# Last expert quad brought back to features as well as rows, its overflow branch moved ahead of it, and two weight splits moved ahead of the convolution's taps

## The reference

```python
def hierarchical_moe(h, ...):              # end of the first layer
    a = jnp.einsum('sd,edf->sef', hr, w_gate)
    u = jnp.einsum('sd,edf->sef', hr, w_up)
    act = jax.nn.silu(a) * u * gate[:, :, None]
    return jnp.einsum('sef,efd->sd', act, w_down)

def hybrid_layer(x, ...):                  # the second layer
    h = rmsnorm(x, g_mix)
    z = h @ w_in
    rnn_x, rnn_y, conv_b, conv_c, conv_x, gate_rnn, gate_conv = jnp.split(z, IN_OFFSETS, axis=-1)
    rnn_x = causal_depthwise_conv(rnn_x, conv4_w) + conv4_b
    y_rnn = jax.nn.gelu(rnn_y) * rg_lru(rnn_x, w_rg_r, b_rg_r, w_rg_i, b_rg_i, lru_lambda)
    y_conv = conv_b * causal_depthwise_conv(conv_c * conv_x, conv3_w)
    merged = jax.nn.sigmoid(gate_rnn) * y_rnn + jax.nn.sigmoid(gate_conv) * y_conv
    x = x + merged @ w_out
```

## Time and profile before

| | us |
|---|---|
| median of 3 runs | 854.52 |
| lowest, highest | 853.46, 856.09 |
| the profiled execution | 852.39 |
| its span, first to last instruction | 850.6 |

### The profile page before, as it was taken

How to read it: one execution, slowest core, us unless ns; L and a number is a source line. 1 busy time by engine, 2 the same in 40 slices (tenths; PEclk the granted TensorE clock), 3 DMA queues, 4 the chain that set the end, 5 groups by cost and what they waited for, 6 DMA issues and landing times.

```text
span 850.6 us, 13779 instructions
## 1 busy us (share of the span) xinstructions
PE 802.4 (94%) x5546; PEld 656.0 (77%) x5546; DVE 493.6 (58%) x832; ACT 416.1 (49%) x708; POOL 20.1 (2%) x41
## 2 busy tenths in 40 slices
PE   9999999999999976788879999999999999999996
PEld 7888888888965543444349899999988888888886
DVE  6667777865542110110047899898976555555486
ACT  5777488666411100100246757575746344444466
POOL 1700000000000000000000000000000000000000
PEclk9999999999999988989999999999999999999999
DMA  9855533977899999999984847465574665655521
GB/s 323 270 192 186 174 112 99 342 300 297 302 384 424 423 425 422 425 423 424 417 284 154 268 127 245 149 221 168 203 253 155 221 188 196 197 170 185 188 99 50
DMA packets 95184, 214.47 MB, mean 252 GB/s; under 512 B 4728, under 2 KB 59552, under 8 KB 81824
## 3 DMA queue, kind: packets, MB, share of 16 engines
q1 hardware_dynamic: 93456, 211.70, 68.3%
q0 software_dynamic: 1376, 1.89, 0.8%
q10 hardware_dynamic: 304, 0.20, 0.1%
HBM read 212.72 MB, written 1.05 MB: 251 GB/s over the span
## 4 chain that ended last, share of the span: by engine, by line
PE 62%; DVE 12%; SPq 11%; DMA 7%; issue 4%; ACT 3%; DVEq 1%; ACTq 0%
PE bank L2212 13%; PE bank L2214 13%; PE bank L2213 13%; SPq L829 11%; DMA embed<-in_expert_w_down_dram 4%; PE bank L2229 4%; PE bank L2225 3%; PE bank L2722 3%; DVE w_lo L455 2%; DVE w_lo L453 2%; PE bank L2219 2%; PE bank L2220 2%; DMA stage<-in_w_in_dram 2%; PE bank L2759 2%; DMA whole<-in_expert_w_down_dram 1%
## 5 line engine op out<-in xcount | busy, mean ns | idle before, releaser
L2212 PE MATMUL bank<-w_hi,xT_hi 128*128 128x512 f32 (+2 forms) x390 | 150.9, 387 | 0.0
L2214 PE MATMUL bank<-w_hi,xT_lo 128*128 128x512 f32 (+2 forms) x390 | 148.5, 381 | 0.0
L2213 PE MATMUL bank<-w_lo,xT_hi 128*128 128x512 f32 (+2 forms) x390 | 148.2, 380 | 0.0
L2954 PE MATMUL bank<-hT_hi,w_hi 128*128 128x256 f32 x440 | 122.2, 278 | 1.7 <-DVE w_lo L455 1.0
L2955 PE MATMUL bank<-hT_lo,w_hi 128*128 128x256 f32 x440 | 121.5, 276 | 0.0
L2956 PE MATMUL bank<-hT_hi,w_lo 128*128 128x256 f32 x440 | 121.5, 276 | 0.0
L453 DVE TENSOR_TENSOR w_lo<-stage,w_hi 128x1024 fp32r<-128x1024 f32 (+3 forms) x78 | 87.8, 1126 | 29.5 <-ACT w_hi L439 28.5
L439 ACT ACTIVATE w_hi<-stage 128x1024 fp32r<-128x1024 f32 (+3 forms) x80 | 78.6, 983 | 26.9 <-PE bank L2214 13.3
L455 DVE TENSOR_TENSOR w_lo<-stage,w_hi 128x1024 fp32r<-128x1024 f32 (+3 forms) x78 | 87.6, 1123 | 0.0
L2954 PEld LDWEIGHTS bank<-hT_hi,w_hi 128*128 128x128 f32 x440 | 82.6, 188 | 2.9 <-DVE w_lo L455 2.1
L2214 PEld LDWEIGHTS bank<-w_hi,xT_lo 128*128 128x128 f32 x390 | 73.3, 188 | 14.2
(11 more groups left out here) (485 smaller groups left out, 1603.2 us busy)
## 6 DMA issues: line engine op xcount, KB each, us to landing
stage<-in_w_in_dram SPq DMA_DIRECT2D x36, 1024.0 KB, 5.4
stage<-in_w_gate_up_dram SPq DMA_DIRECT2D x44, 512.0 KB, 4.7
whole<-in_expert_w_up_dram SPq DMA_DIRECT2D x11, 1024.0 KB, 26.0
stage<-in_w_down_dram SPq DMA_DIRECT2D x11, 1024.0 KB, 4.8
whole<-in_expert_w_gate_dram SPq DMA_DIRECT2D x9, 1024.0 KB, 24.9
stage<-in_w_out_dram SPq DMA_DIRECT2D x8, 1024.0 KB, 5.3
stage<-in_cross_w_kv_dram SPq DMA_DIRECT2D x7, 1024.0 KB, 8.7
whole<-in_expert_w_down_dram SPq DMA_DIRECT2D x6, 1024.0 KB, 23.4
```

The lines of the kernel that those rows point to most:

```text
L2212: mm(o, k_hi, v_hi, start=start, stop=False)
L2213: mm(o, k_hi, v_lo, start=False, stop=False)
L2214: return mm(o, k_lo, v_hi, start=False, stop=stop)
L2954: mm(o, w_hi[:, s, at:at + P], hT_hi[:, k, :], start=k == 0, stop=False)
```

## The change

- The rows' sums of quads 0 to 6 are copied to `x` right after quad 6, turned by `turn_sums` between gates and ups of quad 7, and stay in banks 0 to 3. Quad 7's output is multiplied into those turned banks (`add_turned`: `y` as weights, `token_now` moving, 256 columns) and, apart, into rows in banks 6 and 7 (`rows_back`), which DVE adds to `x` (`add_rows`).
- Banks 0 to 3 then hold the features, so `turn("mix", ...)` goes, and `hT_hi`, `hT_lo` come from them (`mix_high`, `mix_low`). The order of ACT, DVE and PE in the join is written anew. `last_rows` puts the second half of the rows inside `highs_first`.
- The overflow branch and its flag's load go in front of quad 7 on every engine; on SP the head's first three loads come behind it. The four products by `zeros` in it go.
- `x` and `raw_turned` change places in the ring, and units 13 and 20 change order in SP's program.
- In the heads' loop on DVE, `unit(RG_I)` and `unit(G_R)` are put ahead of the `conv3` work and of its second and third taps.

```diff
@@ SP
-        load_expert(sp, 20)
+        load_expert(sp, 13)
         sp.wait_ge(sem("norm_sums"), nth(NORMS, "moe"))
         sp.wait_ge(sem("x_kept"), 4)
-        load_expert(sp, 13)
+        load_expert(sp, 20)
...
-        sp.wait_ge(sem("gates_done"), QUAD * QUADS)
-        for j in range(RING):
-            load_head(0, j)
         with sp.If(over_flag > 0):
...
+        sp.wait_ge(sem("gates_done"), QUAD * QUADS)
+        for j in range(RING):
+            load_head(0, j)
@@ ACT
+        def mix_high(n):
+            act.wait_ge(sem("mix_turned"), n + 1)
+            for j in range(2):
+                k = 2 * n + j
+                ins = nc.scalar.activation(hT_hi[:, k], bank[n][:, 256 * j:256 * j + 256], ACT.Copy, scale=gain_of(MIX_G, k))
+            ins.then_inc(sem("xT_hi"), 1)
...
-        high_parts("mix", MIX_G)
+        down_high(QUADS - 1, 0)
+        mix_high(0)
+        mix_high(1)
+        for t in range(T):
+            mix_squares(0, t)
+        down_high(QUADS - 1, 1)
+        first_columns_hi(0)
+        mix_high(2)
+        mix_high(3)
         first_columns_hi(1)
         split_hi(act, SLOT, U_HEADS + 1)
-        mix_squares(0, 0)
-        mix_squares(0, 1)
         mix_squares(1, 0)
         mix_squares(1, 1).then_inc(sem("norm_sums"), 1)
@@ DVE
+        down_low(QUADS - 1, 0)
+        mix_low(0)
+        mix_low(1)
+        add_rows(0)
+        down_low(QUADS - 1, 1)
+        first_columns_lo(0)
+        mix_low(2)
+        mix_low(3)
         first_columns_lo(1)
+        add_rows(1)
         split_lo(dve, SLOT, U_HEADS + 1)
...
             link(stt(y_in[:], y_tanh[:], 1.0, y_in[:], ALU.add, ALU.mult))
+            unit(RG_I)
...
             for f in range(2):
                 ins = ts(conv3[:, f], cpad[:, f, 0:256], col(conv3_w, 0, f), None, ALU.mult)
+            unit(G_R)
             for tap in range(1, 3):
...
             link(ins)
-            unit(RG_I)
-            unit(G_R)
             unit(G_C)
@@ PE
+        def turn_sums():
+            pe.wait_ge(sem("sums_copied"), 4)
+            view = x[:].rearrange("p t (k q) -> p t k q", k=KD)
+            for n in range(4):
+                for j in range(2):
+                    for t in range(T):
+                        mm(bank[n][:, 256 * j + P * t:256 * j + P * t + P], view[:, t, 2 * n + j], ident, start=j == 0 and t == 0, stop=False, is_transpose=True)
+
+        def add_turned(c, y, low):
+            for n in (2 * c, 2 * c + 1):
+                for j in range(2):
+                    at = 256 * n + P * j - 512 * c
+                    ins = mm(bank[n][:, 256 * j:256 * j + 256], y[:, c, at:at + P], token_now[:].rearrange("p t s -> p (t s)"), start=False, stop=low and j == 1)
+                if low:
+                    ins.then_inc(sem("mix_turned"), 1)
...
+        last = QUADS - 1
+        quad(last)
+        pe.wait_ge(sem("embed_copied"), 4)
+        down(last, 0)
+        pe.wait_ge(sem("token_now"), QUADS)
+        pe.wait_ge(sem("expert_y_hi"), 2 * last + 1)
+        add_turned(0, y_hi, False)
+        rows_back(0, y_hi, False)
+        pe.wait_ge(sem("expert_y_lo"), 2 * last + 1)
+        add_turned(0, y_lo, True)
+        rows_back(0, y_lo, True)
+        down(last, 1)
+        pe.wait_ge(sem("expert_y_hi"), 2 * last + 2)
+        add_turned(1, y_hi, False)
+        pe.wait_ge(sem("expert_y_lo"), 2 * last + 2)
+        add_turned(1, y_lo, True)
...
-        turn("mix", x, [("x_moe0", 1), ("x_moe1", 1)], (0, 1))
-        turn("mix", x, [("x_moe0", 2), ("x_moe1", 2)], (2, 3))
```

More of the change, by code:

```diff
@@ L1355, in expert_quad, with down_high @@
             nc.scalar.activation(hiddenT[:].rearrange("p k s -> p (k s)"), bank[7][:, 0:2 * P], ACT.Copy).then_inc(sem("hidden_copied"), 1)
-            for c in range(2):
-                act.wait_ge(sem("downs_done"), QUAD * (2 * q + c + 1))
-                nc.scalar.activation(y_hi[:, c], bank[4 + c][:, :], ACT.Copy).then_inc(sem("expert_y_hi"), 1)
+            if q < QUADS - 1:
+                for c in range(2):
+                    down_high(q, c)
+        def down_high(q, c):
+            act.wait_ge(sem("downs_done"), QUAD * (2 * q + c + 1))
+            nc.scalar.activation(y_hi[:, c], bank[4 + c][:, :], ACT.Copy).then_inc(sem("expert_y_hi"), 1)
         def embed_copies(t):
@@ L2745, in turn_hidden, with down, downs_here @@
             ins.then_inc(sem("expert_turned"), 1)
-        def down(q):
+        def down(q, c):
             units = [QUAD_UNITS * q + QUAD * 2 + j for j in range(QUAD)]
+            if q == QUADS - 1 and c:
+                pe.wait_ge(sem("last_halves"), 16 * QUAD)
+            for k in range(2):
+                at = D * k + 512 * c
+                for j, i in enumerate(units):
+                    ins = mm(bank[4 + c][strip(j), :], hiddenT[:, k, strip(j)], expert_unit(i)[:, at:at + 512], start=k == 0, stop=k == 1)
+                    if k == 1:
+                        ins.then_inc(sem("downs_done"), 1)
+        def downs_here(q):
             units_here(pe, q, 2)
@@ L2752, in down @@
             pe.wait_ge(sem("rows_ready"), 2 * min(q + 2, QUADS))
-            for c in range(2):
-                if q == QUADS - 1 and c:
-                    pe.wait_ge(sem("last_halves"), 16 * QUAD)
-                for k in range(2):
-                    at = D * k + 512 * c
-                    for j, i in enumerate(units):
-                        ins = mm(bank[4 + c][strip(j), :], hiddenT[:, k, strip(j)], expert_unit(i)[:, at:at + 512], start=k == 0, stop=k == 1)
-                        if k == 1:
-                            ins.then_inc(sem("downs_done"), 1)
         def bring_back(q):
@@ L2793, in embed_products, with quad @@
                 ins.then_inc(sem("embed_filled"), 1)
-        gather(0)
-        for q in range(QUADS):
+        def quad(q):
             columns(q, 0)
             turn_slots(q)
+            if q == QUADS - 1:
+                turn_sums()
             columns(q, 1)
@@ L2802, in _ @@
             turn_hidden(q)
-            if q == QUADS - 1:
-                pe.wait_ge(sem("embed_copied"), 4)
+            downs_here(q)
+        gather(0)
+        for q in range(QUADS - 1):
+            if q == QUADS - 2:
                 over_flag = overflow(pe)
-            down(q)
+            quad(q)
+            for c in range(2):
+                down(q, c)
             bring_back(q)
@@ L2809, in _ @@
                 add_tokens()
[L2810 to L2812 removed]
+        for t in range(T):
+            embed_products(t)
         def overflow_experts():
[L2816 to L2817 removed]
+            pe.wait_ge(sem("embed_copied"), 4)
             for k in range(KD):
@@ L2820, in overflow_experts @@
                     ins = transpose(bank[4 + k // 2][:, 256 * (k % 2) + P * t:256 * (k % 2) + P * t + P], kept[:, t, k])
+                    if (k, t) == (KD - 1, 0):
+                        ins.then_inc(sem("over_started"), 1)
                 ins.then_inc(sem("over_blocks"), 1)
             pe.wait_ge(sem("over_rows"), 1)
-            for n in range(4):
-                ins = mm(bank[n][:, :], zeros[:], y_hi[:, 0], start=True, stop=False)
-            ins.then_inc(sem("over_started"), 1)
             with pe.Fori(0, EXPERTS) as e:
```

163 lines of the change are left out of this document (86 added, 77 removed), and 1 row of the table products.

## The result

| | before | after | ratio, 95% interval |
|---|---|---|---|
| median, us | 854.62 (853.46 to 856.09, 6 runs) | 860.50 (858.67 to 862.79, 6 runs) | 1.0078 (1.0063 to 1.0094) |
| profiled execution, us | 852.39 | 860.90 | |

The change costs 5.9 us, 0.78%. The forecast was 853.5 with a range up to 856.3, so it was wrong in size and in sign.

The account below looks back on a forecast made before the run. PE, busy 94% of the span, was taken as the bound. 0.1 + 0.48 + 0.9 - 2.08 - 0.43 = -1.0 us gave 851.4 from the profiled 852.39, or 853.5 by the runs' median; range 851.2 to 856.3.

Parts of the forecast that it names:

- The step that failed: PE's product stream: a 256-column product costs 0.113 us, 0.114 used, taken from the kernel before.
- Edits at nothing: Ring exchange, dropped products by zero and moved overflow branch: taken as 0, with 0.5 us kept for the branch.
- The starting point: Runs' median 854.52 lies 2.1 us above the profiled 852.39; used to turn 851.4 into 853.5.
- Transposes of the sums: Join: 16 transposes, 1.99 us, move into PE's 2.00 us wait for quad 7's ups; +0.1 us.
- Second half: Join: second `y_hi` 2.25 us later behind two squares on ACT, PE waits 2.9 us; second column starts +0.48 us.
- The join's sum: Join: 0.1 for transposes, 0.48 for the second column's later start, 0.9 for PE's clock.
- The clock's fall: After PE's new 2.9 us wait in the join its granted clock falls again: +0.9 us.
- Heads' waits: Heads: PE's waits for `w_lo` go, gaining 2.08 us in head 0 and 0.43 in the others.
- The branch: Rival: each crossing of the moved overflow branch costs a 1 us instruction fetch; +1.0, 854.5 us, chance 0.07.
- G_R's high part: Rival, heads: ACT's high part isn't there when DVE comes, PE follows DVE's delay; +4.0, 858.5 us, chance 0.08.

Follow-up runs that it names:

- e2: Kernel before with 64 B of unused memory ahead of `rx_hi`, no instruction changed: 859.94 us, ratio 1.0051.
- e16: The whole change with 448 B ahead of `rx_hi`, so the heads' moving operands lie at before's addresses: 851.98 us, ratio 0.9976.
- e9: Kernel before, unchanged, profiled a second time: 854.22 us.
- e18: Changed kernel with before's order in the heads and 448 B ahead of `rx_hi` (join alone, at before's addresses): 857.97 us, ratio 1.0036.
- e5: Changed kernel with before's order in the heads and 64 B ahead of `rx_hi` (join alone): 858.3 us, ratio 1.0048.
- e11: Changed kernel with 128 B of unused memory ahead of `rx_hi`: 859.95 us, ratio 1.0069.
- e1: Changed kernel with 64 B of unused memory ahead of `rx_hi`: 858.79 us, ratio 1.0037.
- e3: Kernel before with only the change's order in the heads (splits of RG_I and G_R ahead of the taps on DVE): 853.07 us, ratio 0.9965.
- e7: Kernel before with 64 B ahead of its first tile, moving weights and moving operands together: 856.01 us, ratio 1.0025.

## Why the prediction was wrong

- **The step that failed** is in its first paragraph: "a product of 256 columns costs 41.82/369 = 0.113 us in a stream", carried from the kernel before to the kernel after as if it belonged to the instruction. It belongs to the place of its operands too. The sum has no term for it, the rivals have none, and the part "Edits at nothing" speaks of the four products by zero (eight in the source) without noting that the tile they used was dropped. Measured: 113.3 ns became 120.0, +9.4 us (shown by e2 and by e16; the heads of e16 take 160.6 us where those of the change take 170.0). Without it the change gives -2.0 where -1.0 was forecast.
- **The starting point.** "The runs' median is 854.52, 2.1 above" the profiled execution: that profile was one with 113.3 ns in all heads, and the second one, 854.22, had 117.8 in a third of them. So the offset of 2.1 was no constant: at least a part of it is the chance of the slower level. In the range, the terms that the prediction names give 851.6 to 855.9; it has 0.4 more on either side without a term.
- **Transposes of the sums: right.** 1.91 us at 423.50, in front of quad 7's ups, with 0.36 of wait left where none was expected.
- **Second half: right in mechanism.** `y_hi` behind the squares, PE's wait 2.52 for 2.9 forecast. From the second downs to head 0's first product it took 6.65 us, 6.88 forecast, 6.10 before.
- **The join's sum: too small in the profile after.** 2.6 where 0.1 + 0.48 + 0.9 = 1.5 was forecast. In after 1.4 of it is the clock, in a place that I had not looked at: the first downs took 3.30 for 1.92, at a granted clock of 0.51. The kernel before has that in some executions too (3.59 in e9), but there the wait of 2.45 us behind them shrank to 0.80 and nothing was lost. The change fills that wait, so the cover is gone. In e16 the first downs took 1.92, and the low clock fell on more of head 0's first products instead (5.84 us to the second column for 4.27 before, 4.42 in after). The Trainium skill ("TensorE: Matmul & The Clock Gate", section "Part 1: The HAM clock gate") says that the moment of change falls differently from run to run; these profiles agree. That both places sum to 2.6 is chance: the same join, by the same two instants, is 1.2 us longer than before in e18, 2.2 in e5 and e11, and 3.7 in e1. The forecast 1.5 lies inside that spread, so one profile could not have judged it.
- **The clock's fall: right**, 0.70 and 0.50 in the windows behind the wait.
- **Heads' waits: right, and worth more.** 4.35 us where 2.51 was forecast. I had summed the waits that the view lists; each also makes the first step behind it some 222 ns long where 113 is normal, and gaps of 0.1 to 0.5 us at 451, 467, 559 and 600 us stand in no list or with less than they cost.
- **The rivals.** The branch: no stall is to be seen at its new place, though it wasn't measured apart. G_R's high part: no wait of PE or longer gap in any head. None of the rivals named the slower end that came.

The three parts at before's addresses, from e3, e18 and e16: order of the heads -0.35%, join +0.36%, both -0.24%. The whole looks better than the sum of the two, but the 0.25 points between them are no more than the three intervals together allow. e16 has fewer gaps in the heads (0.23 us in all) than the order alone (0.96), with 113.3 ns from the first long stretch to the end.

## What to carry to other kernels

Before an edit that adds, drops or moves a tile is timed, compare the addresses of all streaming operands in the two programs; an edit that removes a tile can be undone in place with unused memory, and only then is the order's own worth measured. Read a stream's step (products in a window that holds no wait) in both profiles first: it tells at once whether a difference is in waits or in the rate. A wait that seems free may be the cover for a clock that is sometimes low, and one profile of a kernel whose runs spread by 6 us can show either end of them.

## What the runs showed of the hardware

- **A product's step depends on where its operands lie.** 256 columns in fp32 at a granted clock of 1.00 took 113.3, 117.8 or 120.0 ns with the distance of moving operand and weights at 192, 64 or 0 modulo 256 B (at 192 sometimes 117.8 too), and 213 to 214 ns at 0.50 whatever the distance. The Trainium skill ("TensorE: Matmul & The Clock Gate", section "Wait — 56ns, not 53.3ns?") gives N/1.2 GHz for the low clock, 213.3 for 256 columns, and the trace agrees; for the high one it gives N/2.4 GHz + 2.5 ns for matmuls back to back, by which I estimate 109.2 ns, and no stretch of the heads, where each product loads its weights, was as fast.
- **Weight loads are recorded beside the products.** In the streams above a weight load begins 2 to 4 ns behind each product's start and is recorded with 188 to 192 ns, longer than a step. The Trainium skill ("SBUF — State Buffer", section "A bandwidth-pool intuition that's wrong (but worth ruling out)") gives the weight load a read port of its own, independent of the moving operand's. From that I would not expect the distance to matter; e2, e7 and e16 say that it does. That the two reads meet in the same part of the memory would explain it, but no run shows it.
- **At distance 192 there are two levels, 113.3 and 117.8 ns.** A level lasts at least until the next gap in the stream, 155 us in e16, and the same program shows different ones from execution to execution.
